# Seven block products in place of eight in two chunks of four input-projection units, with the sparse attention on two PSUM banks

## The chip, the cores and the metric

One core of a Trainium2 chip runs the whole program once. The time is the device time of that execution in microseconds (us). The engines named here are PE (TensorE, matrix products), DVE (VectorE), ACT (ScalarE), POOL (GpSimd) and SP (SyncE, which here only issues transfers).

## The reference

Two layers of a streaming encoder with 256 rows of width 2048, all in float32:

```python
for l in range(DEPTH):                       # DEPTH = 2, x is 256 x 2048
    h = rmsnorm(x, norm_mix[l])
    proj = h @ w_in[l]
    qa, ka, va, qi, ki, wi, qb, kb, vb = jnp.split(proj, offsets, axis=-1)
    o_a = dsa_branch(qa, ka, va, qi, ki, wi, bias_a)   # branch A: 8 heads x 128, top 64 keys chosen by an indexer
    o_b = swa_branch(qb, kb, vb, sinks[l], bias_b)     # branch B: 16 heads x 64, a window of 128 keys
    g_a, g_b = jnp.split(jax.nn.sigmoid(h @ w_gate[l]), 2, axis=-1)
    merged = g_a * (o_a @ w_branch_a[l]) + g_b * (o_b @ w_branch_b[l])
    x = x + merged @ w_out[l]
    h = rmsnorm(x, norm_mlp[l])
    x = x + jnp.square(jax.nn.relu(h @ w_up[l])) @ w_down[l]
return rmsnorm(x, final_norm)
```

The indexer scores each key as `sum over 16 heads of w * relu(q_idx . k_idx)`, and branch A attends to the 64 best of them.

## The kernel before

**Chunks and units.** Every weight matrix is cut into chunks of 256 rows (two blocks of 128) by 512 columns. Eight chunks make a unit: 512 output columns for all 256 rows of `x`, gathered in a pair of PSUM banks, `acc[s][0]` and `acc[s][1]`. A layer has 472 chunks: 8 narrow ones (`C_MISC`, index keys and the keys and values of branch B), 80 of the input projection (`C_WIN`, ten units), 48 + 48 of gates and branches, 32 of `w_out` and 256 of the MLP. I write "+n" for the chunk with number n counted from `C_WIN`; unit u of the input projection is +8u to +8u+7. Units 0 and 1 give the index queries, 2 and 3 the queries of branch A, 4 and 5 its keys, 6 and 7 its values, 8 and 9 the queries of branch B.

**A ring of four.** SP loads a chunk into `raw[c % 4]`, as soon as DVE has done chunk c-4. ACT rounds it to float32r (`w_hi`, `split`, L922) when PE has done chunk c-4; DVE subtracts for the rest (`w_lo`, L1350). PE multiplies: activations are kept as such a pair too, and each 128x128x512 product is three matmuls (hi x hi, hi x lo, lo x hi, L578 to L580), so a plain chunk is 12 matmuls of 512 columns. ACT and DVE thus run up to four chunks ahead of PE. All order is written out by hand; each engine runs its own list, and waits on counters.

**Seven products.** A "wide" chunk (`seven_products`, L546 to L548) treats the chunk as a 2x2 matrix of blocks times a 2x2 matrix of blocks and does seven products of 256 columns in place of eight, 21 matmuls in all. DVE first makes the sums of the weight blocks in `raw` (`weight_sums`, three instructions, L1359, L1363, L1365), placed one chunk ahead; then 1792 columns are rounded (`split_wide`, two on ACT, one on DVE, L1371). Sums of the activation blocks (`s_hh` and the like) have to be ready, and four of the seven products gather in two further banks; after the unit ACT copies a quarter (L1186 for the gates) and DVE makes five additions (`add_up_sides`, L1767 to L1775) that put the sides and `acc` together into `stage`. Before the change wide chunks are used in the gates of branch B and the MLP, 166 in all, and none in the input projection.

**Jobs.** Between chunks each engine does pieces of attention (`jobs_after`). A job that PE does after chunk c, ACT and DVE do after splitting chunk c+4 (`AHEAD`). Index scores come from `IDX_AT` on, the choice of keys (`choose`, DVE alone) from `TOPK_AT = C_WIN + 40`, the eight heads of branch A from `A_AT`, one each `A_STEP = 2` chunks: PE `a_logits` (L685), DVE `a_low`, ACT `a_exp` (L1020), DVE `a_probs` and `a_spread`, a transposition through HBM issued by POOL, ACT `a_take_probsT` (L1032), and three heads later PE `a_pv` (L698), ACT `a_o_hi` (L1038), DVE `a_o_lo` (L1571). `a_logits` uses banks `att[0]` and `att[1]` in turn, `a_pv` uses `att[2]`.

**Passing on.** Each of units 0 to 5 is scaled by ACT into `stage` (`take_win`, L1128, ahead of chunk 3 of the next unit), transposed in pieces of 32 by DVE (`spread_block`, L1428), stored to HBM by SP (L342), fetched back in four pieces (L348) and placed by ACT (`place`, L984, after chunk 6 of the next unit). Units 6 and 7 are scaled straight into `va`.

Of the kernel before, what the change touches and what calls it, by code (L numbers as in the profile page):

```python
# [11 lines left out]
P = 128  # L12
# [61 lines left out]
IDX_AT, IDX_STEP, IDX_ROUNDS = C_WIN + 24, 2, 6  # L74
TOPK_AT = C_WIN + 40
A_AT, A_STEP = C_WIN + 56, 2
# [14 lines left out]
GATES_WIDE = NBLK * len(WIDE_GATE)  # L91
G_SUMS = len(WIDE_GATE)
LAYER_WIDE = GATES_WIDE + (GROUPS - 1) * N_WIDE + len(WIDE_UP[2])
LAYER_SIDES = NBLK + 2 * (GROUPS - 1) + 1
U_SUMS = (GROUPS - 1) * NBLK
SHARED = ((0, 1, 2, 3, 4, 5, 8, 9), (-2, -1, 2, 3, 4, 5, 6, 7))
H_SUMS = 4
B11, B22, B21, T1, T3, T2, T4 = range(7)
# [15 lines left out]
def trunk_kernel(nc, x, w_misc, w_main, gains, sinks, rel_bias, onehot, final_gain, bias_rows, out):  # L114
    with ExitStack() as ctx:
# [11 lines left out]
        h_hl = sb("h_hl", [P, 2, KT, SEQ], F32R)  # L127
        o_hl = sb("o_hl", [P, 2, KT, SEQ], F32R)
# [73 lines left out]
        idx_banks = wide_acc  # L202
        first_turn = [acc[0][0], acc[0][1], acc[1][0], acc[1][1], turn, att[2], acc[0][0], acc[0][1]]
# [103 lines left out]
        def _(sp):  # L307
# [215 lines left out]
        def _(pe):  # L523
# [132 lines left out]

            def m_lhs(part, k, t):
                return o_lhs(part, k, t) if k < 8 else m_hl[:, part, k - 8, t * P:(t + 1) * P]


            def idx_scores(l, r):
                if r == 0:
                    pe.wait_ge(placed, l * E_M + (E_QK + 2))
                elif r >= 2:
                    pe.wait_ge(idx_relu, l * IDX_ROUNDS + (r - 1))
                t = 0 if r < 2 else 1
                keys = (t + 1) * P
                heads = NB // keys
                for i in range(heads):
                    for odd in range(2):  # L670
                        j = (r % 2 if t == 0 else r - 2) * heads + i
                        rows = slice(64 * odd, 64 * odd + 64)
                        last = nc.tensor.matmul(idx_banks[r % 2][odd][:, i * keys:(i + 1) * keys],
                                                qiT[rows, j, t * P:(t + 1) * P], kiT_kbT[rows, 0, 0:keys],
                                                start=(i == 0), stop=(i == heads - 1), skip_group_check=True)
                last.then_inc(idx_done, 1)

            def a_logits(l, h):
                if h == 0:
                    pe.wait_ge(placed, l * E_M + (E_QK + 6))  # L680
                    pe.wait_ge(idx_relu, (l + 1) * IDX_ROUNDS)
                if h >= 2:
                    pe.wait_ge(low_ready, l * JOBS + (h - 1))
                b = att[h % 2]
                nc.tensor.matmul(b[:, 0:P], qk[:, 0, h, 0:P], qk[:, 1, h, 0:P], start=True, stop=False, skip_group_check=True)  # L685
                nc.tensor.matmul(b[:, P:3 * P], qk[:, 0, h, P:SEQ], qk[:, 1, h, :], start=False, stop=True,
                                 skip_group_check=True).then_inc(logits_done, 1)

            def a_pv(l, h):
# [7 lines left out]
                b, pT = att[2], probsT[h % 2]  # L697
# [75 lines left out]
            for l in range(DEPTH):  # L773
# [19 lines left out]
                for u in range(N_WIN):  # L793
                    def win_between(c, u=u):
                        if l == 0 and u == 0 and c == 1:
                            spread_rows()
                        jobs_after(l, C_WIN + 8 * u + c)

                    def win_before(u=u):
                        if u >= 2:  # L800
                            pe.wait_ge(act_took, l * ACT_UNITS + (u - 1))
                    unit(l * CHUNKS + (C_WIN + 8 * u), 8, h_lhs, acc[u % 2], win_between, win_before)
# [75 lines left out]
                for g in range(GROUPS - 1):  # L878
                    up(g * 64 + (C_MLP + 16), 0, up_two_before(g), 2, [(1, h_sums_took, (G_SUMS + H_SUMS) * (l + 1))], WIDE_UP[2])
# [36 lines left out]
        def _(act):  # L916
# [119 lines left out]
            def a_o_hi(l, h):  # L1036
                act.wait_ge(pv_done, l * JOBS + (h + 1))
                nc.scalar.activation(o_hl[:, 0, h, :], att[2][:, 0:SEQ], ACT.Copy).then_inc(o_hi, 1)  # L1038
# [67 lines left out]
            for l in range(DEPTH):  # L1106
# [26 lines left out]

                def take_rows():
# [16 lines left out]
                for u in range(N_WIN):  # L1151
                    unit(l * CHUNKS + (C_WIN + 8 * u), 8,
                         take=(lambda u=u: take_win(u - 1)) if u else take_misc, taken=win_place(u),
                         jobs=win_jobs(u))
# [10 lines left out]
                def gate_sums_hi(n):  # L1165
                    act.wait_ge(h_summed, l * (G_SUMS + H_SUMS) + n + 1)
# [21 lines left out]
                def gate_tanh(n):  # L1188
                    act.wait_ge(up_summed, l * LAYER_SIDES + n + 1)
# [4 lines left out]
                def gate_steps(n):  # L1194
                    return lambda i: 3 * (l * LAYER_WIDE + n * len(WIDE_GATE) + i + 1)
# [11 lines left out]
                def h_sums(n):  # L1207
                    act.wait_ge(h_summed, l * (G_SUMS + H_SUMS) + G_SUMS + n + 1)
# [60 lines left out]
                def sides_count(g, i):  # L1269
                    return g * 2 + (l * LAYER_SIDES + NBLK + i + 1)  # L1270
# [72 lines left out]
        def _(dve):  # L1343
# [194 lines left out]
            def a_low(l, h):  # L1538
# [12 lines left out]
                low_of(att[h % 2], p, p[:, 0:P], 0, 0)  # L1551
                low_of(att[h % 2], p, p[:, P:3 * P], 1, 1).then_inc(low_ready, 1)
# [131 lines left out]
            for l in range(DEPTH):  # L1684
# [13 lines left out]

                for u in range(N_WIN):
                    take = take_keys if u == 0 else (lambda u=u: take_stage(u - 1)) if u <= 6 or u == 9 else None  # L1700
                    unit(l * CHUNKS + (C_WIN + 8 * u), 8, take=take, jobs=lambda c, u=u: jobs_after(l, C_WIN + 8 * u + c - AHEAD))
# [24 lines left out]
                def gate_sums(n):  # L1726

                    hi, lo = (h_hl[:, part, PIECES * n + 2:PIECES * n + 4, :].rearrange("p k s -> p (k s)").bitcast(F32)
                              for part in range(2))
                    both = stage2[:, 1, :]  # L1730
                    a11, a21, a12, a22 = (both[:, i * P:(i + 1) * P] for i in range(4))
                    s1, s2, s3, s4 = (sums_f[:, i * P:(i + 1) * P] for i in range(4))
                    chain.link(nc.vector.tensor_tensor(both, hi, lo, ALU.add))
                    nc.vector.tensor_tensor(s3, a21, a11, ALU.subtract)
                    chain.link(nc.vector.tensor_tensor(s1, a21, a22, ALU.add))
                    chain.link(nc.vector.tensor_tensor(s2, s1, a11, ALU.subtract))
                    nc.vector.tensor_tensor(s4, a12, s2, ALU.subtract).then_inc(h_summed, 1)

                def gate_sums_lo(n):
                    dve.wait_ge(h_sums_hi, l * (G_SUMS + H_SUMS) + n + 1)  # L1740
# [19 lines left out]
                def add_up_sides(g, n, i):  # L1760

                    z, w = wide_acc[n // 2]
                    at = g * 2 + (l * LAYER_SIDES + i)
                    steps = g * 6 + 3 * (l * LAYER_SIDES + i)
                    quarters = stage[:].rearrange("p t (h c) -> p (t h) c", h=2)
                    dve.wait_ge(sides_out, at + 1)
                    nc.vector.tensor_tensor(side_sum, z[:, 0:HALF], quarters[:, 1, :], ALU.add).then_inc(up_step, 1)  # L1767
                    dve.wait_ge(up_step, steps + 1)
                    nc.vector.tensor_tensor(quarters[:, 0::3, :], side_sum.unsqueeze(1).to_broadcast([P, 2, HALF]),
                                            w[:].rearrange("p (h c) -> p h c", h=2), ALU.subtract).then_inc(up_step, 1)  # L1770
                    dve.wait_ge(up_step, steps + 2)
# [56 lines left out]
                def h_sums(n):  # L1828
                    dve.wait_ge(h_sums_hi, l * (G_SUMS + H_SUMS) + G_SUMS + n + 1)
# [260 lines left out]
```

## Time and profile before

| | us |
|---|---|
| median of 3 runs (lowest to highest) | 2659.84 (2659.27 to 2660.45) |
| the profiled execution | 2658.03 |
| its span, first to last instruction | 2656.1 |
| PE busy in it | 2641.4 |
| DVE busy | 2078.8 |
| ACT busy | 1448.1 |
| granted TensorE clock | 0.999 |

The page shows one execution, with 1.9 us outside its span. A matmul's own duration (0.39 us for 512 columns) is longer than its distance from the next, because matmuls overlap in the array; what a chunk costs is read from start to start.

### The profile page before, as it was taken

To read this page: it belongs to the slowest core of one execution; us is meant where nothing else is said; L and a number is where in the kernel's file an instruction comes from. 1 tells how busy PE (TensorE), PEld (TensorE's weight loads), DVE (VectorE), ACT (ScalarE), POOL (GpSimd) and SP (SyncE) were. 2 spreads that over 40 slices of the span, in tenths; PEclk is the share of its full clock that TensorE was granted. 3 is DMA by queue.
4 is the path that set the end of the run, shared out by engine and by line. 5 is a ranking of instruction groups with operands and counts; after the bars stand their busy time and mean duration, and the time that the engine had idled before them with its cause. 6 is when DMAs were issued, how large, how long until landed. Compare 5 with 4: busy or idle time off the path is not lost.

```text
span 2656.1 us, 37301 instructions
## 1 busy us (share of the span) xinstructions
PE 2641.4 (99%) x13432; PEld 2217.1 (83%) x13432; DVE 2078.8 (78%) x3099; ACT 1448.1 (55%) x1863; POOL 215.8 (8%) x378
## 2 busy tenths in 40 slices
PE   9999999999999999999999999999999999999998
PEld 7788778888888888888888887788888888888887
DVE  5667678967898897987756766789678989989875
ACT  5445555545565655655455455555456556556554
POOL 0103110000100100100010021100000001000000
PEclk9999999999999999999999999999999999999999
DMA  7877676666775766767777666667677767667574
GB/s 260 239 236 224 222 226 195 229 231 231 244 228 191 246 216 206 240 205 232 235 237 225 224 225 221 218 202 233 227 256 231 221 208 242 209 217 234 189 248 151
DMA packets 187395, 594.52 MB, mean 224 GB/s; under 512 B 25576, under 2 KB 46612, under 8 KB 187088
## 3 DMA queue, kind: packets, MB, share of 16 engines
q1 hardware_dynamic: 166256, 536.94, 62.1%
q0 software_dynamic: 20432, 54.86, 7.5%
q8 instruction: 106, 1.74, 0.3%
q14 instruction: 73, 0.60, 0.1%
q10 hardware_dynamic: 528, 0.37, 0.1%
HBM read 544.58 MB, written 47.48 MB: 223 GB/s over the span
## 4 chain that ended last, share of the span: by engine, by line
PE 95%; DVE 3%; DMA 1%; issue 1%; ACT 0%; DVEq 0%; POOLq 0%; POOL 0%; SPq 0%; ACTq 0%
PE acc L578 24%; PE acc L579 24%; PE acc L580 24%; PE att L546 2%; PE att L548 2%; PE att L547 2%; PE acc L546 2%; PE acc L548 2%; PE acc L547 2%; PE acc L595 1%; PE acc L594 1%; PE acc L596 1%; DMA raw<-in_w_main 1%; DVE w_lo L1350 1%; DVE w_lo L1371 1%
## 5 line engine op out<-in xcount | busy, mean ns | idle before, releaser
L1350 DVE TENSOR_TENSOR w_lo<-raw,w_hi 128x1024 fp32r<-128x1024 f32 (+1 forms) x778 | 933.2, 1211 | 374.0 <-ACT w_hi L922 370.3
L922 ACT ACTIVATE w_hi<-raw 128x1024 fp32r<-128x1024 f32 (+1 forms) x778 | 813.1, 1051 | 633.5 <-PE acc L580 462.4
L578 PE MATMUL acc<-w_hi,h_hl 128*128 128x512 f32 x1848 | 735.2, 398 | 1.1 <-DVE w_lo L1350 1.1
L580 PE MATMUL acc<-w_hi,h_hl 128*128 128x512 f32 x1848 | 728.9, 394 | 0.0
L579 PE MATMUL acc<-w_lo,h_hl 128*128 128x512 f32 x1848 | 728.6, 394 | 0.0
L578 PEld LDWEIGHTS acc<-w_hi,h_hl 128*128 128x128 f32 x1848 | 347.9, 188 | 83.0 <-issue 4.9
L580 PEld LDWEIGHTS acc<-w_hi,h_hl 128*128 128x128 f32 x1848 | 347.9, 188 | 81.3
L579 PEld LDWEIGHTS acc<-w_lo,h_hl 128*128 128x128 f32 x1848 | 348.2, 188 | 76.3
L1371 DVE TENSOR_TENSOR w_lo<-raw,w_hi 128x1792 fp32r<-128x1792 f32 x166 | 335.5, 2021 | 33.5 <-ACT w_hi L931 32.4
L578 PE MATMUL acc<-w_hi,o_hl 128*128 128x512 f32 x912 | 360.4, 395 | 0.0
L579 PE MATMUL acc<-w_lo,o_hl 128*128 128x512 f32 x912 | 360.0, 395 | 0.0
L580 PE MATMUL acc<-w_hi,o_hl 128*128 128x512 f32 x912 | 359.6, 394 | 0.0
L929 ACT ACTIVATE w_hi<-raw 128x768 fp32r<-128x768 f32 x166 | 140.3, 845 | 195.0 <-PE acc L548 110.1
L931 ACT ACTIVATE w_hi<-raw 128x1024 fp32r<-128x1024 f32 x166 | 174.9, 1054 | 86.9 <-DVE raw L1365 86.7
L580 PEld LDWEIGHTS acc<-w_hi,o_hl 128*128 128x128 f32 x912 | 171.8, 188 | 40.2
L578 PEld LDWEIGHTS acc<-w_hi,o_hl 128*128 128x128 f32 x912 | 171.6, 188 | 37.7 <-issue 1.4
L579 PEld LDWEIGHTS acc<-w_lo,o_hl 128*128 128x128 f32 x912 | 171.7, 188 | 36.3
L1359 DVE TENSOR_TENSOR raw<-raw 128x512 f32<-128x512 f32 x166 | 113.3, 683 | 21.2 <-issue 11.3
L455 POOL DMA_DIRECT2D scratch<-spread x30 | 16.9, 563 | 973.2 <-DVE spread L1428 973.2
L1428 DVE STREAM_TRANSPOSE spread<-stage 128x512 f32<-128x512 f32 x112 | 73.0, 689 | 21.8 <-ACT stage L1128 17.5
L1020 ACT ACTIVATE probs<-probs,low 128x128 f32<-128x128 f32 x96 | 41.0, 428 | 85.0 <-DVE sink_d L1592 43.8
L1363 DVE TENSOR_TENSOR raw<-raw 128x256 f32<-128x256 f32 x166 | 70.6, 425 | 5.8
(298 smaller groups left out, 3614.9 us busy)
## 6 DMA issues: line engine op xcount, KB each, us to landing
raw<-in_w_main SPq DMA_DIRECT2D x928, 512.0 KB, 4.3
scratch<-spread SPq DMA_DIRECT2D x37, 512.0 KB, 2.8
moved<-scratch SPq DMA_DIRECT2D x148, 128.0 KB, 3.2
scratch<-spread POOLq DMA_DIRECT2D x30, 512.0 KB, 3.5
moved<-scratch POOLq DMA_DIRECT2D x120, 128.0 KB, 5.0
scratch_p<-spread POOLq DMA_DIRECT2D x16, 384.0 KB, 4.6
moved<-scratch_p POOLq DMA_DIRECT2D x64, 96.0 KB, 4.3
raw<-in_w_misc SPq DMA_DIRECT2D x16, 336.0 KB, 4.0
```

Of the source, the lines that this page charges most:

```text
L546: nc.tensor.matmul(o, a_hi, hi[:, w], start=start, stop=False, skip_group_check=True)
L547: nc.tensor.matmul(o, a_hi, lo[:, w], start=False, stop=False, skip_group_check=True)
L548: return nc.tensor.matmul(o, a_lo, hi[:, w], start=False, stop=stop, skip_group_check=True)
L578: nc.tensor.matmul(o, a_hi, hi[:, kk], start=(k == 0), stop=False)
L579: nc.tensor.matmul(o, a_hi, lo[:, kk], start=False, stop=False)
L580: last = nc.tensor.matmul(o, a_lo, hi[:, kk], start=False, stop=fin)
L922: nc.scalar.activation(w_hi[s][:, 0:2 * width], raw[r][:, 0:2 * width], ACT.Copy).then_inc(hi_ready, 1)
L929: nc.scalar.activation(w_hi[s][:, 0:3 * HALF], raw[s][:, HALF:CW], ACT.Copy)
L931: nc.scalar.activation(w_hi[s][:, 3 * HALF:7 * HALF], raw[s][:, CW:2 * CW], ACT.Copy).then_inc(hi_ready, 1)
L1350: nc.vector.tensor_tensor(w_lo[s][:, 0:2 * width], raw[r][:, 0:2 * width], w_hi[s][:, 0:2 * width].bitcast(F32), ALU.subtract).then_inc(lo ...
L1359: nc.vector.tensor_tensor(r[:, 4 * HALF:6 * HALF].rearrange("p (k n) -> p k n", k=2), r[:, HALF:3 * HALF].rearrange("p (k n) -> p k n", k= ...
L1371: nc.vector.tensor_tensor(w_lo[s][:, 0:7 * HALF], raw[s][:, HALF:8 * HALF], w_hi[s][:, 0:7 * HALF].bitcast(F32), ALU.subtract).then_inc(lo ...
```

## The change

Units 1, 2, 6 and 7 of the input projection (`WIN_UNITS`) do their chunks 1 and 5 (`WIN_CHUNKS`) as seven products: 8 chunks per layer, 16 in all. Their side products gather in `att[0]`, `att[1]` (units 1 and 6) and `att[2]`, `turn` (units 2 and 7). Since branch A would then meet unit 7's sides, its logits all use `att[0]` and its outputs `att[1]`; each `a_logits` so waits for the `low_ready` of the head before. The index scores begin four chunks later, the heads of branch A two chunks later. Unit 0 gets the sums of the activations (`gate_sums`, moved ahead in the file, and `win_sums_lo`). The results of units 1 and 2 are spread after chunk 5 of the next unit in place of ahead of chunk 3, and passed on and placed in the unit after it. The index keys, `best8`, the activation sums and a side sum lie in the half of `o_hl` that is not yet used, since `raw1` now needs its full width.

```diff
-IDX_AT, IDX_STEP, IDX_ROUNDS = C_WIN + 24, 2, 6
+IDX_AT, IDX_STEP, IDX_ROUNDS = C_WIN + 28, 2, 6
-A_AT, A_STEP = C_WIN + 56, 2
+A_AT, A_STEP = C_WIN + 58, 2
+WIN_UNITS = (1, 2, 6, 7)
+WIN_CHUNKS = (1, 5)
...
+        s_win = o_hl[:, :, 10:14, :].rearrange("p a k s -> p a (k s)").rearrange("p a (b c) -> p a b c", b=W_SUMS)
...
+        win_sides = dict(zip(WIN_UNITS, (wide_acc[0], wide_acc[1], wide_acc[0], wide_acc[1])))
...
# SP, for each unit u
+                    if u - 2 in WIN_UNITS[0:2]:
+                        store, fetch = pass_on(l, E_QK + u - 2)
+                        then = {1: [store], 2: [fetch]}
+                    load_unit(l, C_WIN + 8 * u, 8, None if u - 1 in WIN_UNITS[0:2] else passing, then=then)
...
# PE
+                    pe.wait_ge(up_summed, l * LAYER_SIDES + 2)          # idx_scores, first round
...
-                if h >= 2:
-                    pe.wait_ge(low_ready, l * JOBS + (h - 1))
-                b = att[h % 2]
+                    pe.wait_ge(up_summed, l * LAYER_SIDES + 3)          # a_logits, h == 0
+                else:
+                    pe.wait_ge(low_ready, l * JOBS + h)
+                b = att[0]
...
-                b, pT = att[2], probsT[h % 2]
+                b, pT = att[1], probsT[h % 2]
...
+                    hold = {1: [(1, misc_took, l + 1), (1, h_sums_took, l * LAYER_SUMS + 1), (5, h_sums_took, l * LAYER_SUMS + 2)],
+                            2: [(1, rows_out, 1)], 6: [(1, idx_relu, (l + 1) * IDX_ROUNDS)]}
...
# ACT
+                def win_side(u):
+                    unit_done(l * CHUNKS + (C_WIN + 8 * (u + 1)))
+                    act.wait_ge(spread_ready, l * MOVES + (E_QK + min(u, 6)))
+                    nc.scalar.activation(stage[:, 0, HALF:NB], win_sides[u][0][:, HALF:NB], ACT.Copy).then_inc(sides_out, 1)
+
+                def win_scale(u):
+                    act.wait_ge(up_summed, l * LAYER_SIDES + WIN_UNITS.index(u) + 1)
+                    for t in range(TT):
+                        dst = stage[:, t, :] if u < 6 else va[:, t, (u - 6) * NB:(u - 5) * NB]
+                        last = nc.scalar.activation(dst, stage[:, t, :], ACT.Copy, scale=rms[:, 2 if u == 2 else 0, t:t + 1])
+                    last.then_inc(act_took, 1)
...
+                    if u == 0:
+                        then = {5: lambda: win_sums_hi(0), 7: lambda: win_sums_hi(1)}
+                    if was_wide:
+                        then[4] = lambda u=u: win_scale(u - 1)
+                    if u - 2 in WIN_UNITS[0:2]:
+                        then[0] = win_place(u - 1)
...
# DVE
+                    if u == 0:
+                        then = {4: lambda: gate_sums(0), 6: first_lo_second_sums}
+                    if u == 1:
+                        then = {0: lambda: win_sums_lo(1)}
+                    if u - 1 in WIN_UNITS:
+                        then[3] = lambda u=u: add_win_sides(u - 1)
+                        if u <= 6:
+                            then[5] = take
+                        take = None
```

`then[k]` is done after the split of chunk k of the unit.

**What moves on ACT around unit 7 and the heads of branch A.** Names: `w_hi` is a split, `probs` a head's exponentials (two rows a head), `probsT` the transposed probabilities of an earlier head, `o_hl<-att` an output of `a_pv`, `qiv` the values. Before, from the last rows of one head to the next:

```order
L1020 ACTIVATE probs,den<-probs,low 128x256
L1032 ACTIVATE probsT<-moved_a 128x384
L922 ACTIVATE w_hi<-raw 128x1024 x2
L1038 ACTIVATE o_hl<-att 128x256
L1020 ACTIVATE probs,den<-probs,low 128x128
L1020 ACTIVATE probs,den<-probs,low 128x256
L1032 ACTIVATE probsT<-moved_a 128x384
L1128 ACTIVATE qiv<-acc,rms 128x512 x2
```

and of the changed kernel, the same heads:

```order
L1055 ACTIVATE probsT<-moved_a 128x384
L1160 ACTIVATE stage<-att 128x256
L945 ACTIVATE w_hi<-raw 128x1024 x2
L1166 ACTIVATE qiv<-stage,rms 128x512 x2
L1061 ACTIVATE o_hl<-att 128x256
L1043 ACTIVATE probs,den<-probs,low 128x128
L1043 ACTIVATE probs,den<-probs,low 128x256
L1055 ACTIVATE probsT<-moved_a 128x384
```

The copy of the side (L1160) and the scaling of unit 7's values (L1166) now stand inside the chain of head 3: ahead of its output copy, its exponentials and head 1's `probsT`.

**What moves on DVE at the same place.** Names: `w_lo` a split, `win_side_sum` and `stage` the five additions of a side, `o_hl<-att` an output of branch A. Before, ahead of head 3:

```order
L1566 STREAM_TRANSPOSE stage<-probs 128x3x4x32
L1350 TENSOR_TENSOR w_lo<-raw,w_hi 128x1024 x2
L1571 TENSOR_TENSOR o_hl<-att,o_hl 128x256
L1545 TENSOR_TENSOR probs<-bias_a,score 128x128
L1546 TENSOR_TENSOR probs<-bias_a,score 128x256
```

and changed, up to the head's output and first row (head 3 goes on behind it as before):

```order
L1617 STREAM_TRANSPOSE stage<-probs 128x3x4x32
L1401 TENSOR_TENSOR w_lo<-raw,w_hi 128x1024
L1782 TENSOR_TENSOR win_side_sum<-att,stage 128x256
L1784 TENSOR_TENSOR stage<-win_side_sum,turn 128x2x256
L1787 TENSOR_TENSOR stage<-stage,turn 128x256
L1788 TENSOR_TENSOR stage<-acc,stage 128x512
L1790 TENSOR_TENSOR stage<-acc,stage 128x512
```

The five additions stand between the two splits that lead to head 3.

**What moves on ACT in units 2 and 3.** `qiv<-moved` is the placing of index queries. Before, it stands after seven splits of the unit that follows, here with the taking of the unit ahead of it:

```order
L1128 ACTIVATE stage<-acc,rms 128x512 x2
L922 ACTIVATE w_hi<-raw 128x1024 x4
L984 ACTIVATE qiv<-moved 128x1024
L922 ACTIVATE w_hi<-raw 128x1024 x4
```

and of the changed kernel, for the second of the two:

```order
L1160 ACTIVATE stage<-att 128x256
L945 ACTIVATE w_hi<-raw 128x1024 x2
L1166 ACTIVATE stage<-stage,rms 128x512 x2
L952 ACTIVATE w_hi<-raw 128x768
L954 ACTIVATE w_hi<-raw 128x1024
L945 ACTIVATE w_hi<-raw 128x1024 x3
L1007 ACTIVATE qiv<-moved 128x1024
```

Six chunks are now split between the unit's end and the placing, two more than the four before.

## Rows read from the trace of the kernel before

**Rows 1.** The page: the span, the engines' busy time.
```profile
span 2656.1 us, 37301 instructions
PE 2641.4 (99%) x13432; PEld 2217.1 (83%) x13432; DVE 2078.8 (78%) x3099; ACT 1448.1 (55%) x1863; POOL 215.8 (8%) x378
```
**Rows 2.** Waits of PE: us in total, times, longest.
```profile
PE acc L578 <- DVE w_lo L1350: 1.1, 1, 1.1
```
**Rows 3.** PE in order of time (start, duration): a wide chunk, then a plain one.
```profile
725.87 0.28 PE L546 MATMUL att<-w_hi,s_hh 128*128 128x256 f32 x1
...
728.35 0.39 PE L578 MATMUL acc<-w_hi,h_hl 128*128 128x512 f32 x1
...
731.13 0.28 PE L546 MATMUL att<-w_hi,s_hh 128*128 128x256 f32 x1
```
**Rows 4.** One form of weight load on PE: ns min/median/max, first and last start.
```profile
L546 PEld LDWEIGHTS att<-w_hi,s_hh x182: 186/188/192, 419.2 to 2533.1; 128*128 128x128 f32 x182
```
**Rows 5.** Split of one plain chunk (+4 of layer 0): ACT, DVE, PE.
```profile
53.60 1.06 ACT L922 ACTIVATE w_hi<-raw 128x1024 fp32r<-128x1024 f32 x1 [0.65 <-PE acc L580]
54.70 1.22 DVE L1350 TENSOR_TENSOR w_lo<-raw,w_hi 128x1024 fp32r<-128x1024 f32 x1 [0.24 <-ACT w_hi L922]
61.74 0.40 PE L578 MATMUL acc<-w_hi,h_hl 128*128 128x512 f32 x1
```
**Rows 6.** DVE in a gate unit: additions of the sides, weight sums, split, wide split.
```profile
440.40 0.42 DVE L1767 TENSOR_TENSOR stage<-att,stage 128x256 f32<-128x256 f32 x1
...
443.11 0.68 DVE L1359 TENSOR_TENSOR raw<-raw 128x512 f32<-128x512 f32 x1
...
444.63 1.22 DVE L1350 TENSOR_TENSOR w_lo<-raw,w_hi 128x1024 fp32r<-128x1024 f32 x1
446.28 2.02 DVE L1371 TENSOR_TENSOR w_lo<-raw,w_hi 128x1792 fp32r<-128x1792 f32 x1 [0.44 <-ACT w_hi L931]
```
**Rows 7.** ACT there: copy of the side, scaling of the unit.
```profile
437.90 0.39 ACT L1186 ACTIVATE stage<-att 128x256 f32<-128x256 f32 x1 [1.36 <-PE acc L548]
...
443.23 1.34 ACT L1191 ACTIVATE stage<-stage,rms 128x512 f32<-128x512 f32 x2 [1.43 <-DVE stage L1775]
```
**Rows 8.** DVE, ACT and PE in branch A, layer 0, by time.
```profile
209.72 0.39 PE L578 MATMUL acc<-w_hi,h_hl 128*128 128x512 f32 x1
210.00 0.08 DVE L1535 DVE_READ_ACCUMULATOR2_ANT low<- 128x1 f32 x1
212.50 2.58 DVE L1350 TENSOR_TENSOR w_lo<-raw,w_hi 128x1024 fp32r<-128x1024 f32 x2
215.00 0.42 DVE L1571 TENSOR_TENSOR o_hl<-att,o_hl 128x256 fp32r<-128x256 f32 x1
217.56 0.51 ACT L1032 ACTIVATE probsT<-moved_a 128x384 f32<-128x384 f32 x1
219.39 0.59 PE L698 MATMUL att<-probsT,qiv 128*128 128x256 f32 x2
```
**Rows 9.** Passing on: transposition on DVE (page); slowest and fastest of twelve passes.
```profile
L1428 DVE STREAM_TRANSPOSE spread<-stage 128x512 f32<-128x512 f32 x112 | 73.0, 689 | 21.8 <-ACT stage L1128 17.5
...
1392.57 0.33 SPq L342 DMA_DIRECT2D scratch<-spread  x1
1403.41 1.06 ACT L984 ACTIVATE qiv<-moved 128x1024 f32<-128x1024 f32 x1 [3.99 <-DMA moved<-scratch]
1465.91 0.33 SPq L342 DMA_DIRECT2D scratch<-spread  x1
1473.81 1.06 ACT L984 ACTIVATE qk<-moved 128x1024 f32<-128x1024 f32 x1 [1.05 <-DMA moved<-scratch]
```
**Rows 10.** DVE and PE at the choice of keys, unit 6.
```profile
176.09 1.23 DVE L1350 TENSOR_TENSOR w_lo<-raw,w_hi 128x1024 fp32r<-128x1024 f32 x1
182.66 0.39 PE L578 MATMUL acc<-w_hi,h_hl 128*128 128x512 f32 x1
```
**Rows 11.** Busy time by stretch (us, then PE, PEld, DVE, ACT, POOL).
```profile
416.00:560.00 144.00, 144.00 (x785) 124.38 (x784) 126.94 (x144) 77.04 (x84) 3.53 (x1) 1.00 0.68 223
```

More of the change, by code:

```diff
@@ L1037, in a_o_hi @@
                 act.wait_ge(pv_done, l * JOBS + (h + 1))
-                nc.scalar.activation(o_hl[:, 0, h, :], att[2][:, 0:SEQ], ACT.Copy).then_inc(o_hi, 1)
+                nc.scalar.activation(o_hl[:, 0, h, :], att[1][:, 0:SEQ], ACT.Copy).then_inc(o_hi, 1)
             def b_exp(l, j):
@@ L1151, in _ @@
                 for u in range(N_WIN):
+                    was_wide, then = u - 1 in WIN_UNITS, {}
+                    if u == 0:
[4 more added lines that the diff above has]
+                        then[0] = win_place(u - 1)
                     unit(l * CHUNKS + (C_WIN + 8 * u), 8,
-                         take=(lambda u=u: take_win(u - 1)) if u else take_misc, taken=win_place(u),
-                         jobs=win_jobs(u))
+                         take=(lambda u=u: win_side(u - 1)) if was_wide else (lambda u=u: take_win(u - 1)) if u else take_misc,
+                         taken=None if u - 1 in WIN_UNITS[0:2] else win_place(u), jobs=win_jobs(u), then=then,
+                         wide=WIN_CHUNKS if u in WIN_UNITS else (),
+                         steps=early_steps(WIN_UNITS.index(u)) if u in WIN_UNITS else None)
                 def take_gate(cl_end, branches):
@@ L1697, in take_stage, with gate_sums @@
                     spread_block(l, E_QK + u if u < 6 else E_QB + u - 8, stage)
+                def gate_sums(n):
+                    hi, lo = (h_hl[:, part, PIECES * n + 2:PIECES * n + 4, :].rearrange("p k s -> p (k s)").bitcast(F32)
+                              for part in range(2))
+                    both = stage2[:, 1, :]
+                    a11, a21, a12, a22 = (both[:, i * P:(i + 1) * P] for i in range(4))
+                    s1, s2, s3, s4 = (sums_f[:, i * P:(i + 1) * P] for i in range(4))
+                    chain.link(nc.vector.tensor_tensor(both, hi, lo, ALU.add))
+                    nc.vector.tensor_tensor(s3, a21, a11, ALU.subtract)
+                    chain.link(nc.vector.tensor_tensor(s1, a21, a22, ALU.add))
+                    chain.link(nc.vector.tensor_tensor(s2, s1, a11, ALU.subtract))
+                    nc.vector.tensor_tensor(s4, a12, s2, ALU.subtract).then_inc(h_summed, 1)
@@ L1724, in take_branch_b @@
                     spread_block(l, E_M + n, stage2)
[L1726 to L1737, printed above, removed]
                 def gate_sums_lo(n):
-                    dve.wait_ge(h_sums_hi, l * (G_SUMS + H_SUMS) + n + 1)
+                    dve.wait_ge(h_sums_hi, l * LAYER_SUMS + W_SUMS + n + 1)
                     nc.vector.tensor_tensor(s_hh[:, 1, n, :], sums_f, s_hh[:, 0, n, :].bitcast(F32), ALU.subtract)\
```

103 lines of the change are left out of this document (67 added, 36 removed).

## Prediction

> **What bounds the kernel now.** I first read the page's busy times [rows 1]: the reader is to see that PE is busy for 2641.4 us of a span of 2656.1, and DVE for 2078.8. PE sets the time, and DVE is the engine nearest behind it. Then PE's waits [rows 2]: in the whole span it once waited for a split, for 1.1 us. So work taken from PE is a gain at once, and work given to DVE or ACT costs nothing until PE meets something that isn't ready. The rest of the reading was to find where that happens: what a chunk costs PE [rows 3], how far ahead its split is ready [rows 5], and what stands in series in the places where the order moves [rows 6 to 10].
>
> **What PE saves.** A wide chunk lasts from 725.87 to 728.35, 2.48 us, the plain one behind it from 728.35 to 731.13, 2.78 to 2.79 [rows 3]. I use 2.79, so 0.31 is saved. Four units with two such chunks in two layers are 16 chunks: 16 x 0.31 = 4.96 us. That is 0.19% of the time, and this measurement can tell about 0.2% (5.3 us) from no change. So even with the whole gain the kernel would hardly be told to be faster.
>
> A wide chunk has 21 matmuls in place of 12, so nine more weight loads. Such a load lasts 0.188 us [rows 4], and 21 of them would be 3.95 us in a row, more than the 2.48 us that the whole chunk lasts [rows 3]: they lie beside the matmuls. The Trainium skill ("TensorE: Matmul & The Clock Gate", section "Measured speedup vs the span model") says that a weight load overlaps matmuls in flight only when its row group differs; all of these loads use all 128 rows. By that rule the nine loads would stand in series, 16 x 9 x 0.188 = 27 us more, and the change would lose some 22 us. The trace disagrees, by the two durations above.
>
> **What is added beside PE.** On DVE: the sums of the weight blocks 1.52 us per wide chunk (443.11 to 444.63), the wide split 2.02 in place of 1.22, so 0.80, and the additions of the sides 2.71 per unit (440.40 to 443.11) [rows 6]. On ACT: a copy of 0.39 per unit; the scaling, 1.34, was there before, and moves from the unit's end to behind the additions [rows 7]. The activation sums of unit 0 are new work for DVE and ACT, about 2.7 us twice and 0.4 us twice by rows of such sizes (two or three operations like those of rows 6, one like that of rows 7).
>
> A normal split is ready long before its use: that of chunk +4 ends at 55.92, and PE starts the chunk at 61.74, 5.8 us later [rows 5]. It can hardly be earlier, since a slot comes free only when PE is done with it. So at each place there is a cover of up to 5.8 us, and an addition below it is free. For unit 0 and for the first wide chunks that holds with 2 to 3 us left, and I cost them at nothing. In the stretch of gate units that are built in this way, DVE is busy for 126.94 of 144.00 us and PE for all 144.00 [rows 11]: such a load alone doesn't stall PE. What can is a place where several things stand in series. I find three.
>
> **Place A: head 3 and unit 7's sides.** Zero is PE's start of the chunk after which it does the first output of branch A: 209.72 before [rows 8]. Before, by those rows: DVE starts the two splits at +2.78 (212.50), head 0's output is at +5.28 (215.00), and the `probsT` of head 1 is ready at +8.35 (217.56 + 0.51). PE comes for it at +9.67 (219.39). The margin is 1.32 us. In the changed order unit 7's sides, scaling and all, stand ahead of that `probsT`:
> - DVE comes 0.7 late from the wide chunk and the sides ahead of it. That is a choice: 1.52 + 0.80 + 0.31 = 2.63 are added there, and there are idle stretches that take up most of it; between 0 and 1.5.
> - ACT's copy of the side, 0.39, ahead of the split: it starts at 2.78 + 0.7 + 0.39 = 3.87, and ends 1.2 later at 5.07.
> - Five additions, 2.71: 7.78. ACT's scaling waits for them, 1.34: 9.1. Behind it on ACT stands the output copy of head 0, which DVE waits for, 0.39 by the copy of the same size: 9.5.
> - From that output on the order is as before, 8.35 - 5.28 = 3.07: `probsT` is ready at 12.6.
>
> PE comes at 9.67 (the three chunks up to there are plain in both), so it waits 2.9 us, in each of two layers: +5.8. The bounds are those of the lateness: with 0 it is 2.2, with 1.5 it is 3.7 per layer. Behind ACT's late instructions the splits of the next chunks queue as well, but their cover is larger, and PE itself is held. Head 4's logits stand on PE behind this wait, so their new wait for head 3's `low` (on DVE about 1.3 us behind the output, 10.9) costs nothing further.
>
> **Place B: index queries placed late.** Zero is PE's start of +16, the first chunk of unit 2. DVE does the additions of unit 1 up to about 5.5 (ACT copies the side and rounds +19, DVE splits it until 2.8, then 2.71), weight sums to 7.0, the split of +20 to 8.2, the wide split of +21 to 10.65, and the two transpositions (2 x 0.689 [rows 9]) to 12.0. Then the pass through HBM: from SP's store to ACT's placing it took 7.9 us in the fastest (1465.91 to 1473.81) and 10.84 in the slowest (1392.57 to 1403.41) [rows 9]. I take 9.5, near the middle: 21.5. The placing is 1.06, and behind it on ACT stands the rounding of +25, 1.06, then DVE's split, 1.22 [rows 5]: 24.8. PE wants +25 at 6 x 2.79 + 2 x 2.48 + 2.79 = 24.49. So about 0.4 us per layer, with bounds of 0 (a pass of 7.9) and 1.7 (one of 10.84): +0.8. Unit 2's own placing is one unit later, where no wide chunk hastens PE; its cover is larger, and I cost it at nothing.
>
> This pass is a store and a fetch. The Trainium skill ("DMA: Bandwidth & Descriptors", section "Anatomy of one DMA — SWDGE (gpsimd) path") gives about 2 us of fixed cost for a transfer, two of them 4 us; by an estimate from that, place B would have no wait at all and the sum would be 0.8 lower. The fastest pass of this trace, 7.9 us, disagrees, so I go by the rows.
>
> **Place C: the choice of keys.** Here DVE has no gap. Its split ends at 177.32 and PE starts the chunk at 182.66: 5.34 left [rows 10]. Unit 6 adds 2 x (1.52 + 0.80) = 4.64 ahead of it, PE comes 0.31 earlier, and the scores are some 0.1 later: 0.3 is left. I take 0.1 per layer, +0.2, with bounds of 0 and, if DVE comes 1 us late from the unit before, 0.7.
>
> **The sum.** -4.96 + 5.8 + 0.8 + 0.2 = +1.84. The profiled execution lasted 2658.03, of which 1.9 lie outside the span, and would become 2659.9. The median is 1.8 above that execution, 2659.84, and becomes 2661.7. With places A to C at their lower bounds the sum is -4.96 + 4.4 = -0.6 (2659.3), at their upper -4.96 + 7.4 + 3.4 + 1.4 = +7.2 (2667.1).
>
> **The rivals.**
> - The whole gain: no wait surfaces, 2659.84 - 4.96 = 2654.9. For it speaks that in the gate units DVE carries the same load with no stall of PE [rows 11]; against it that head 3's chain has but 1.32 us of margin [rows 8], and 4.5 us are put into it. It would need DVE and ACT to have idle time in this chain that I haven't seen.
> - The slower side: DVE comes to unit 6 and unit 8 about 1.5 us later than I take it, because between +48 and +66 it gets 2 x 2.71 + 4 x 2.32 = 14.7 us more work beside the choice of keys, which has no gaps. Then A costs 3.7 and C 0.7 or more per layer, and with B at the upper half (1.0) the sum is -4.96 + 7.4 + 1.4 + 2.0 = +5.8, with a split or two more that come late about +7: 2667. It decides from about 1 us of lateness at +53.
> - One bank for the logits: each head's logits wait for the `low` of the head before. Before, head 2's was read at 210.08, and the next logits could come at the earliest after the chunk, at 209.72 + 2.79 = 212.51 [rows 8], so 2.43 us of margin. If DVE were later than that at every head, by 0.5 us say, the 14 such waits would cost 7 us: 2668.7. Against it: the lateness of 0.7 doesn't use the margin up.
> - Weight loads in series, as above, some 2682: the rows speak against it.
>
> **How the numbers follow.** The forecast, waits at A of about 2.9 and small ones at B and C, has 0.56, with its own range of 2659.3 to 2664.5. The whole gain, or most of it, has 0.14; DVE behind by more 0.21; the logits' wait 0.06; loads or anything unlike these 0.03. Faster by over 0.2% is below 2654.5: even the whole gain ends just above it, so 0.06, from the first rival. Slower by over 0.2% is above 2665.2: most of the second and third, and the edge of the forecast, 0.26. Within it 0.68. The range is 2655.2 to 2668: it leaves out a little of each side.
>
> **What would show it.** In the profile after, a wide chunk of the input projection should last 2.48 us. PE should wait at `a_pv` of head 1 for ACT's `probsT`, twice, 2.9 us each; a wait of under 1 us there makes place A wrong, and with it the forecast. At +25 it should wait for `w_lo` by 0 to 1.7, at +53 by 0 to 0.7. DVE's busy time should grow by 16 x 2.32 + 8 x 2.71 + 4 x 2.7 = 70 us, to some 2149. PE waits at other splits of units 6 to 8 would speak for the second rival, and waits of the logits for `low` for the third.

## The result, and the profile after

| | before | changed |
|---|---|---|
| median (lowest to highest), us | 2659.56 (2656.28 to 2661.04), 6 runs | 2678.11 (2675.30 to 2681.02), 6 runs |
| profiled execution's span | 2656.1 | 2678.5 |
| PE busy | 2641.4 | 2648.8 |
| DVE busy | 2078.8 | 2141.5 |
| granted TensorE clock | 0.999 | 0.997 |

The ratio is 1.0071, 95% interval 1.0059 to 1.0082: slower, by 18.6 us. Forecast were 2661.7 and a range up to 2668.0.

The page of the changed kernel, against [rows 1]:

```profile
span 2678.5 us, 37743 instructions
PE 2648.8 (99%) x13576; PEld 2226.0 (83%) x13576; DVE 2141.5 (80%) x3211; ACT 1461.4 (55%) x1891; POOL 215.7 (8%) x378
```

The span grew by 22.4 us. PE's idle time in it grew from 14.7 (2656.1 - 2641.4) to 29.7, so by 15.0, and its busy time by 7.4, though 4.96 us of work were to go. So PE also ran slower somewhere. PE's waits, in us, times, longest (answers to [rows 2]):

```profile
PE acc L593 <- DVE w_lo L1401: 6.0, 6, 3.0
PE att L718 <- ACT probsT L1055: 5.4, 2, 2.7
PE att L692 <- ACT stage L1037: 4.4, 3, 1.8
...
PE att L561 <- DVE w_lo L1422: 1.2, 2, 0.9
```

The second row is place A of the prediction. The first is mostly place B: 4.7 of its 6.0 us are two waits, at +25 of each layer; of the other four the longest is 0.5. The third is in no step of it: L692 are the index scores, waiting for ACT to take the round before out of the banks. Here are PE's rows at the five waits of units 3 and 4 (chunks +25, +32, +36 of layer 0, +25 and +36 of layer 1), the bracket telling the idle time and its releaser:

```profile
100.86 0.51 PE L593 MATMUL acc<-w_hi,h_hl 128*128 128x512 f32 x1 [1.65 <-DVE w_lo L1401]
...
128.48 0.48 PE L692 MATMUL att<-kiT_kbT,qiv 64*128 64x256 f32 x1 [1.80 <-ACT stage L1037]
...
145.27 0.48 PE L692 MATMUL att<-kiT_kbT,qiv 64*128 64x256 f32 x1 [1.70 <-ACT stage L1037]
...
1430.25 0.79 PE L593 MATMUL acc<-w_hi,h_hl 128*128 128x512 f32 x1 [3.05 <-DVE w_lo L1401]
...
1471.76 0.48 PE L692 MATMUL att<-kiT_kbT,qiv 64*128 64x256 f32 x1 [0.92 <-ACT stage L1037]
```

Together 9.1 us. Why, ACT's rows of the same stretch say (start, duration, bracket as above):

```profile
97.54 1.06 ACT L1007 ACTIVATE qiv<-moved 128x1024 f32<-128x1024 f32 x1 [8.03 <-DMA moved<-scratch]
98.51 1.99 ACT L945 ACTIVATE w_hi<-raw 128x1024 fp32r<-128x1024 f32 x2
...
122.18 1.06 ACT L1007 ACTIVATE qk<-moved 128x1024 f32<-128x1024 f32 x1 [8.74 <-DMA moved<-scratch]
123.15 1.07 ACT L1037 ACTIVATE stage<-att 128x512 f32<-128x512 f32 x2
...
143.19 1.06 ACT L1007 ACTIVATE qk<-moved 128x1024 f32<-128x1024 f32 x1 [5.09 <-DMA moved<-scratch]
144.15 0.58 ACT L1037 ACTIVATE stage<-att 128x512 f32<-128x512 f32 x1
```

L1007 is the placing, of units 1, 2 and 3. ACT stands at it for 8.03, 8.74 and 5.09 us, and what is queued behind it is what PE wants: first the split of +25, then twice the take of index scores (L1037). In the kernel before the first take was done at 99.45, nine us ahead of unit 2's placing:

```profile
99.45 1.09 ACT L1014 ACTIVATE stage<-att 128x512 f32<-128x512 f32 x2
...
108.93 1.06 ACT L984 ACTIVATE qk<-moved 128x1024 f32<-128x1024 f32 x1 [1.71 <-DMA moved<-scratch]
```

For units 1 and 2 SP's rows show the store and, behind a chunk's load, the fetch (4 pieces), in layer 0:

```profile
86.36 0.33 SPq L353 DMA_DIRECT2D scratch<-spread  x1
...
90.73 1.75 SPq L359 DMA_DIRECT2D moved<-scratch  x4
...
110.61 0.33 SPq L353 DMA_DIRECT2D scratch<-spread  x1
...
116.19 1.75 SPq L359 DMA_DIRECT2D moved<-scratch  x4
```

From store to placing that is 11.18 and 11.57 us.

And PE ran slower behind some of these waits. The stretches behind those of 128.48 and 145.27, and one between them (PE busy and count, PEld, DVE, ACT, POOL, then the granted clock, DMA share, GB/s):

```profile
130.00:134.00 4.00, 4.00 (x13) 3.08 (x12) 3.75 (x10) 2.56 (x4) 0.60 (x1) 0.62 0.93 278
134.00:138.00 4.00, 4.00 (x19) 3.25 (x18) 3.89 (x6) 2.02 (x2) 0.60 (x1) 1.00 0.78 271
147.00:150.00 3.00, 3.00 (x8) 2.30 (x7) 2.96 (x4) 1.20 (x3) 0.26 (x1) 0.50 0.21 50
```

A clock of 0.50 is TensorE at its lower level, 1.2 GHz. From start to start, chunk +33 then took 4.45 us, +37 4.44, and +25 of layer 1 4.39, where 2.89 is normal behind such jobs: 4.6 us for three chunks. Behind the wait of 1.65 at +25 of layer 0 the chunk took its normal 2.89.

Place A, with PE, ACT and DVE by time (answers to [rows 8]; PE's start of +64 is at 224.25):

```profile
229.56 0.41 DVE L1782 TENSOR_TENSOR win_side_sum<-att,stage 128x256 f32<-128x256 f32 x1
231.67 0.68 DVE L1790 TENSOR_TENSOR stage<-acc,stage 128x512 f32<-128x512 f32 x1
232.39 1.34 ACT L1166 ACTIVATE qiv<-stage,rms 128x512 f32<-128x512 f32 x2 [3.05 <-DVE stage L1790]
234.03 0.42 DVE L1622 TENSOR_TENSOR o_hl<-att,o_hl 128x256 fp32r<-128x256 f32 x1 [0.55 <-ACT o_hl L1061]
236.59 0.51 ACT L1055 ACTIVATE probsT<-moved_a 128x384 f32<-128x384 f32 x1
237.15 0.70 PE L718 MATMUL att<-probsT,qiv 128*128 128x256 f32 x2 [2.71 <-ACT probsT L1055]
```

The output of head 0 is at +9.78 (forecast 9.5), `probsT` at +12.85 (12.6), and PE waits 2.71 in layer 0 and 2.64 in layer 1 (2.9). PE itself came later too, at +10.2 (9.67), so two small misses cancel in part.

### The profile page after: what moved, and what is told of

It is laid out like the page before. It is cut to its first block, busy times and chain, and to the rows that moved or that the text cites. A ratio compares the mean times of both kernels' runs of the same rounds, so it can differ in the third digit from the quotient of the medians.

```text
span 2678.5 us, 37743 instructions
## 1 busy us (share of the span) xinstructions
PE 2648.8 (99%) x13576; PEld 2226.0 (83%) x13576; DVE 2141.5 (80%) x3211; ACT 1461.4 (55%) x1891; POOL 215.7 (8%) x378
## 4 chain that ended last, share of the span: by engine, by line
PE 75%; DVE 12%; DMA 6%; issue 4%; ACT 2%; SPq 1%; POOL 0%; DVEq 0%; POOLq 0%; ACTq 0%
PE acc L593 18%; PE acc L595 18%; PE acc L594 18%; DVE w_lo L1401 4%; DMA raw<-in_w_main 2%; PE att L561 2%; PE att L563 2%; PE att L562 2%; DMA moved<-scratch 2%; PE acc L561 2%; PE acc L563 2%; PE acc L562 2%; DMA scratch<-spread 2%; DVE w_lo L1422 1%; PE acc L611 1%
## 5 line engine op out<-in xcount | busy, mean ns | idle before, releaser
L1401 DVE TENSOR_TENSOR w_lo<-raw,w_hi 128x1024 fp32r<-128x1024 f32 (+1 forms) x762 | 912.4, 1210 | 312.7 <-ACT w_hi L945 310.9
L945 ACT ACTIVATE w_hi<-raw 128x1024 fp32r<-128x1024 f32 (+1 forms) x762 | 793.0, 1050 | 539.8 <-PE acc L595 348.6
L593 PE MATMUL acc<-w_hi,h_hl 128*128 128x512 f32 x1784 | 712.5, 399 | 6.3 <-DVE w_lo L1401 6.0
L595 PE MATMUL acc<-w_hi,h_hl 128*128 128x512 f32 x1784 | 705.4, 395 | 0.0
L594 PE MATMUL acc<-w_lo,h_hl 128*128 128x512 f32 x1784 | 705.3, 395 | 0.0
L593 PEld LDWEIGHTS acc<-w_hi,h_hl 128*128 128x128 f32 x1784 | 336.9, 189 | 87.9 <-DVE w_lo L1401 9.0
L595 PEld LDWEIGHTS acc<-w_hi,h_hl 128*128 128x128 f32 x1784 | 336.9, 189 | 79.0
L1422 DVE TENSOR_TENSOR w_lo<-raw,w_hi 128x1792 fp32r<-128x1792 f32 x182 | 367.9, 2021 | 30.8 <-ACT w_hi L954 30.0
L952 ACT ACTIVATE w_hi<-raw 128x768 fp32r<-128x768 f32 x182 | 153.7, 845 | 201.5 <-PE acc L563 102.2
L954 ACT ACTIVATE w_hi<-raw 128x1024 fp32r<-128x1024 f32 x182 | 191.9, 1055 | 108.7 <-DVE raw L1416 108.5
L1410 DVE TENSOR_TENSOR raw<-raw 128x512 f32<-128x512 f32 x182 | 124.3, 683 | 33.9 <-DMA raw<-in_w_main 22.2
L1414 DVE TENSOR_TENSOR raw<-raw 128x256 f32<-128x256 f32 x182 | 77.4, 425 | 6.3
L1416 DVE TENSOR_TENSOR raw<-raw 128x256 f32<-128x256 f32 x182 | 77.4, 425 | 6.3
```

The costliest lines, as they stand in the source:

```text
L593: nc.tensor.matmul(o, a_hi, hi[:, kk], start=(k == 0), stop=False)
L594: nc.tensor.matmul(o, a_hi, lo[:, kk], start=False, stop=False)
L595: last = nc.tensor.matmul(o, a_lo, hi[:, kk], start=False, stop=fin)
L945: nc.scalar.activation(w_hi[s][:, 0:2 * width], raw[r][:, 0:2 * width], ACT.Copy).then_inc(hi_ready, 1)
L952: nc.scalar.activation(w_hi[s][:, 0:3 * HALF], raw[s][:, HALF:CW], ACT.Copy)
L954: nc.scalar.activation(w_hi[s][:, 3 * HALF:7 * HALF], raw[s][:, CW:2 * CW], ACT.Copy).then_inc(hi_ready, 1)
```

## The experiments

My theory (theory 1): most of the loss comes from the placings on ACT, which stand ahead of splits and index takes while the transfer isn't there, and from the clock that falls behind the waits. The rival (theory 2): it comes from the index rounds being four chunks later, or from DVE being behind with its new work. The kernel before ran beside each; its medians were 2658.69 in the first four, 2659.67 in the others.

**e1, placings later on ACT.**

```diff
-                        then[0] = win_place(u - 1)
+                        then[2 if u == 3 else 3] = win_place(u - 1)
```

> The changed kernel with one edit: ACT places the output of unit 1 after split +26 in place of +24, and that of unit 2 after split +35 in place of +32. Theory 1 (ACT stands at the placing, waiting for a transfer, and the splits and index takes queued behind it come late; TensorE's clock falls behind the pauses): the waits near +25, +32 and +36 and the low clock behind them go, 14.6 us in both layers of the trace after, so about 2663.5 us. Theory 2 (the index rounds themselves, four chunks later, meet unit 3's transfer and the scores on DVE): only the waits at +25 go, about 6 us, so 2672 us, and waits for the index takes stay.

Measured: 2666.9 us (2661.15 to 2672.83), ratio 1.0035 (1.0024 to 1.0046), so 11.2 us less than the changed kernel, or 10.3 if each is compared with the kernel before that ran beside it. The execution with the profile was the fastest of the seven; what the slower ones waited for isn't shown. Its waits:

```profile
PE att L718 <- ACT probsT L1055: 5.8, 3, 2.7
...
PE acc L593 <- DVE w_lo L1401: 1.1, 2, 0.8
PE att L692 <- ACT stage L1037: 1.0, 1, 1.0
```

Waits for splits fell from 6.0 to 1.1 us (both that are left stand behind the input projection), those for the takes from 4.4 to 1.0, at +36, behind unit 3's placing, which this edit leaves where it was. No chunk of units 3 and 4 ran at the lower clock. The first take now stands ahead of unit 2's placing, and the transfer has come when ACT gets there (no bracket on L1007):

```profile
109.29 1.09 ACT L1037 ACTIVATE stage<-att 128x512 f32<-128x512 f32 x2
...
120.84 1.06 ACT L1007 ACTIVATE qk<-moved 128x1024 f32<-128x1024 f32 x1
```

The gain alone doesn't decide: 10 to 11 us lie between the 14.6 of theory 1 and the 6 of theory 2. The waits do, in this trace: theory 2 wanted those for the takes to stay, and they went but for one.

**e2, the index rounds alone, four chunks later, in the kernel before.**

```diff
-IDX_AT, IDX_STEP, IDX_ROUNDS = C_WIN + 24, 2, 6
+IDX_AT, IDX_STEP, IDX_ROUNDS = C_WIN + 28, 2, 6
```

> The kernel before with one edit: the index rounds begin at +28 in place of +24. Theory 1: no wait of PE for the takes, 2659 to 2661 us. Theory 2: PE waits for them at +32 or +36 in each layer, and the clock falls behind it, 4 to 8 us slower than before.

Measured: 2659.51, ratio 1.0001 (0.9993 to 1.001), and no wait of PE for the takes in its trace. The shift alone costs nothing; theory 2 in its first form falls.

**e3, unit 7's additions out of head 3's chain.**

```diff
 # DVE, unit 8
-                        then[3] = lambda u=u: add_win_sides(u - 1)
+                            gaps = {5: lambda: add_win_sides(7, (0,)), 7: lambda: add_win_sides(7, (1,))}
 # ACT
-                        then[4] = lambda u=u: win_scale(u - 1)
+                        then[7 if u == 8 else 4] = lambda u=u: win_scale(u - 1)
```

`gaps` is done ahead of the split of that chunk; part 0 is the first three additions, part 1 the last two.

> The changed kernel with unit 7's five additions out of head 3's chain: three on DVE ahead of split +69, two ahead of +71, the scaling on ACT after split +71. If place A is what the prediction says, PE's wait for probsT (2 x 2.7 us) goes, and 2673 us are left. Rival: DVE and ACT are behind in general there, and the wait moves to another head; no gain.

Measured: 2676.68 (2672.77 to 2682.52), ratio 1.006 (1.0047 to 1.0073): 1.4 us less than the changed kernel, within the spread of both. In the trace:

```profile
PE acc L593 <- DVE w_lo L1401: 7.6, 5, 2.7
PE att L692 <- ACT stage L1037: 5.5, 3, 3.9
PE att L718 <- ACT probsT L1055: 3.6, 4, 1.6
```

The wait behind +66 is gone, but two others stand in its place in each layer, 0.2 behind +68 and 1.6 behind +70. I had moved the scaling ahead of the split of +72, and so into another head's chain. The two upper rows, mostly of units 3 and 4, were longer in this execution, the slowest of the five, than in that of the changed kernel and hide what was won.

**e4, both edits.**

> Both edits together. Theory 1: 14.6 + 5.4 us less than the changed kernel, 2658 us, within 0.2% of the kernel before, on the faster side of it if nothing new waits. Theory 2: some 2666 us.

Measured: 2662.43, ratio 1.0014 (1.0006 to 1.0023), 4.5 us less than e1. What is left in its trace is PE's wait for `probsT` at `a_pv` (3.7 us in five) and, in layer 1, a placing that I hadn't touched, unit 0's. ACT stood at it for 7.25 us, and PE waited 1.78 and 1.68 us for the splits behind it, +15 and +16.

**e5, e4 with ACT's order mended further.** The scaling of unit 7 goes ahead of split +73, and the placings of units 0 and 3 go one split back, behind the index takes:

```diff
+                    if u in (1, 4):
+                        then[7] = win_place(u)
...
+                         at={1: lambda: win_scale(7)} if u == 9 else (),
```

> The kernel with both edits (placings later, unit 7's additions in the gaps), and two more: the scaling of unit 7 on ACT ahead of split +73 in place of after +71, and the placings of units 0 and 3 one split later, behind the index takes. If ACT's order in these places is all that is left, the waits at pv after +70 (1.8 us in each layer), at +36 (1.0 to 1.3) and at +15 go, some 6 us less than 2662.4: 2656 to 2657, ratio 0.999. If DVE is what is late in branch A, the wait at pv stays and the time with it, 2660 or more.

Measured: 2662.57, ratio 1.001 (1.0001 to 1.0019). That missed: I expected 2656 to 2657, and what came is the outcome that I had given for DVE being late in branch A. The waits at the takes and the 1.6 behind +70 are gone, but the heads now wait a little each:

```profile
PE att L718 <- ACT probsT L1057: 2.9, 8, 0.7
```

The one chain that I measured in branch A has 1.32 us to spare [rows 8]. That unit 7's 2.71 + 1.34 us fit into none of them, cut up or not, is how I read it, after two other orders of that work (that of e3 and e4, and that of e5). Which engine is late first isn't shown, since e3 moves work on ACT and on DVE at once.

**e6, seven products in units 1 and 2 alone; e7, in units 6 and 7 alone.**

```diff
-WIN_UNITS = (1, 2, 6, 7)
+WIN_UNITS = (1, 2)       # e6, with A_AT = C_WIN + 56
+WIN_UNITS = (6, 7)       # e7, with IDX_AT = C_WIN + 24 and units 1, 2 passed on as before
```

> The changed kernel with seven products in units 1 and 2 alone (units 6 and 7 plain, branch A's heads back at +56, one bank for the logits as in the changed kernel). Theory 1 (the late placings carry the loss): -2.5 us of PE and the whole of the waits and the slow clock at +25 to +37, 14.6 us: about 2671 us. Rival (DVE behind in units 6 to 8 carries it): no more than 2662 us. If one bank for the logits costs something, waits of the logits for DVE's low show.

Measured: 2671.37 (2666.23 to 2673.48), ratio 1.0043 (1.0029 to 1.0057), as theory 1 has it. Its waits are those of units 3 and 4 alone; the logits, which use one bank here too, wait nowhere:

```profile
PE att L692 <- ACT stage L1036: 8.0, 3, 3.4
PE acc L593 <- DVE w_lo L1400: 4.4, 2, 2.2
```

> The changed kernel with seven products in units 6 and 7 alone, units 1 and 2 plain and passed on and placed as before the change, index rounds from +24. Theory 1: -2.5 us, and +5.8 of the wait at place A and nothing else: about 2662 us, ratio 1.0012. Rival: waits at the splits of unit 6 and more, 2668 us.

Measured: 2667.42, ratio 1.0035 (1.0021 to 1.0048). No wait but the forecast one was to come, and in the input projection only one other did, 0.35 us at the first `a_pv`, yet the time is 5 us above what I expected. PE's row behind the wait and the stretch around it:

```profile
227.36 1.22 PE L717 MATMUL att<-probsT,qiv 128*128 128x256 f32 x2 [2.72 <-ACT probsT L1054]
```

```profile
226.00:230.00 4.00, 2.64 (x9) 2.37 (x9) 3.00 (x6) 3.47 (x8) 0.58 (x1) 0.61 0.07 30
```

The same wait as in the changed kernel (2.72 against 2.71), the same matmuls: 1.22 us here, 0.70 there. The clock fell, and chunk +66 with its jobs took 4.1 us more than before in place of 3.0, in both layers. Twice 4.1, less 2.5 for eight wide chunks, makes 5.7 of the 7.8 between the medians. PE's two waits for splits of over 0.5 us, 1.7 together, stand in the MLP of layer 1, which this edit doesn't touch and where the kernel before has one of 1.09, so they say nothing of units 6 and 7:

```profile
1823.10 0.51 PE L593 MATMUL acc<-w_hi,h_hl 128*128 128x512 f32 x1 [0.76 <-DVE w_lo L1400]
...
2080.32 0.39 PE L561 MATMUL att<-w_hi,m_hl 128*128 128x256 f32 x1 [0.89 <-DVE w_lo L1421]
```

**e8, e6 with the placings later.**

> Units 1 and 2 alone, with ACT's placings after split +26 and +35. Theory 1: the waits at +25, +32 go, 2656 to 2659 us, as the kernel before or 2 us faster. Rival (the transfers themselves are late and keep PE waiting wherever they are placed): 2665 us or more.

Measured: 2659.0, ratio 1.0 (0.9991 to 1.0009), 12.4 us less than e6. PE's waits for takes and splits are down to 0.6 and 0.6 us. The 0.6 for a take stands at +36, behind the placing of unit 3, and the 0.6 for a split in the MLP. The one edit of e1, in a kernel with no other trouble, takes away the loss of units 1 and 2. Of the 2.5 us that eight wide chunks save 0.7 show in the medians, with an interval of 2.4 to either side. The rival (transfers that are late wherever they are placed) falls.

**e9, units 1, 2 and 6, with all four placings later; e10, the same with the heads from +56.**

```diff
-WIN_UNITS = (1, 2, 6, 7)
+WIN_UNITS = (1, 2, 6)
-A_AT, A_STEP = C_WIN + 58, 2        # e10 only
+A_AT, A_STEP = C_WIN + 56, 2
```

> Seven products in units 1, 2 and 6 (unit 7 plain, so no additions stand in a head's chain), ACT's placings later as in e1, those of units 0 and 3 one split later too, heads from +58. By what the runs so far showed no wait of PE over 1 us should be left in units 2 to 8, and 12 wide chunks save 3.7 us: 2655 to 2656 us, ratio 0.9986. If what is left over in units 6 to 8 comes from DVE's load and not from unit 7's sides, waits at pv stay and the time is 2659 or more.

Measured: 2656.52 (2652.65 to 2657.43), ratio 0.9989 (0.9980 to 0.9998): faster than both kernels, by 0.1% against the kernel before, with an interval that ends just short of no change. In units 1 to 9 PE waits for nothing. Its page:

```profile
span 2650.7 us, 37641 instructions
PE 2637.4 (99%) x13540; PEld 2219.6 (84%) x13540; DVE 2129.2 (80%) x3189; ACT 1460.6 (55%) x1885; POOL 215.8 (8%) x378
```

The whole list of its waits:

```profile
PE att L593 <- DVE h_hl L1464: 1.9, 1, 1.9
PE acc L544 <- DMA xs<-in_x: 1.5, 1, 1.5
PE att L785 <- DVE moved L1705: 1.3, 1, 1.3
PE att L593 <- DVE w_lo L1403: 0.3, 1, 0.3
```

PE's busy time is 4.0 below before [rows 1], where 12 chunks by 0.31 make 3.7. So the wide chunks save what was worked out, once nothing waits; the medians differ by 3.2.

> The same with branch A's heads from +56 as before the change. If the first head has to wait for unit 6's additions, it costs 0.5 to 2 us per layer against e9 (2656 to 2660); if not, the same as e9.

Measured: 2664.01, ratio 1.0018 (1.0008 to 1.0027), 7.5 us above e9; I had given 0.5 to 2 per layer. The first head's logits wait for unit 6's additions, 2.7 in each layer, and the clock falls behind that too:

```profile
195.26 0.46 PE L705 MATMUL att<-qk 128*128 128x128 f32 x2 [2.69 <-DVE stage L1792]
```

```profile
194.00:198.00 4.00, 2.74 (x8) 2.28 (x9) 3.42 (x10) 1.84 (x5) 0.00 (x0) 0.70 0.57 168
```

Chunk +57 then took 4.36 us in layer 0 and 4.52 in layer 1, where 2.98 is normal with its jobs. Waiting makes 5.4 us and the clock some 2.9; the sum, 8.3, is near the 7.5 between the medians.

## Why the prediction was wrong, step by step

- **What PE saves, 4.96 us: right.** The wide chunks of the input projection last 2.48 to 2.53 us in the trace after where no head's job stands before them, and in e9 PE's busy time fell by the whole saving. That weight loads lie beside matmuls holds too. (The rule of the Trainium skill that the prediction sets against it stands in "TensorE: Matmul & The Clock Gate", section "The mechanism", and not in the section that the prediction names.) DVE's busy time grew by 62.7 us, where 70 were forecast.
- **Place A, 2.9 us of waiting per layer: right** in the chain (12.85 for 12.6) and the wait (2.71 and 2.64), with PE 0.5 us later than I had it. Its price can be higher than the wait: in e7 it was 4.1 per layer, by the clock.
- **Place C, the choice of keys: right.** The split of +53 was ready 0.50 us ahead of PE in layer 0 (forecast 0.3), and PE didn't wait for it. In e5 and e10 it waited there once, 0.4 and 0.2 us, within the bounds.
- **Place B, 0.4 us per layer: the mechanism was right and the size off.** It was 1.65 and 3.05. The passes took 11.18 (store at 86.36, placing at 97.54) and 11.31 us, outside of the 7.9 to 10.84 of [rows 9], where I had taken 9.5. In layer 1 the store also came later, 13.1 us after PE's start of +16 in place of 12.0; ACT had stood for 6.42 us at the placing of unit 0 before, and that this is the reason isn't shown. The estimate beside it, 4 us for a store and a fetch, takes a figure that the Trainium skill ("DMA: Bandwidth & Descriptors", section "Anatomy of one DMA — SWDGE (gpsimd) path") gives for transfers issued by GpSimd. Here SP issues them, and the six passes of units 1 to 3 took 8.4 to 11.6 us.
- **"Unit 2's own placing is one unit later ...; its cover is larger, and I cost it at nothing": this step failed.** Of what is queued behind the waiting placing I had looked at the splits alone. But ACT's take of the index scores stands there too, ahead of the split, and PE's next round waits for it; before, the take came first. With a pass of 11.57 us in layer 0 unit 2's placing became late, and PE waited 1.80 us for a take. The takes, begun four chunks later, then met unit 3's placing as well, which is in no step at all: 1.70 and 0.92 us. The later start alone costs nothing (e2), and in layer 1 unit 2's pass took 9.44 us and made no wait. e1 and e8 took nearly all of these waits away by placing units 1 and 2 later (1.05 and 0.61 are left, at +36 of layer 0), and e9, which also places unit 3 behind the takes, has none.
- **The clock was in no term of the sum.** Three chunks behind waits cost 4.6 us more. With the two failures above: 4.4 (takes) + 3.9 (place B, 4.7 less 0.8) + 4.6 = 12.9 us. By the starts of PE's chunks the input projection of the two layers took 17.0 us more in the profiled execution (10.1 and 6.9), 15.1 more than the sum's +1.84. The 12.9 are most of that; a chunk also grew by 0.1 to 0.3 us more than the wait in it (+36 of layer 0 by 1.95 for 1.70).
- **What stands outside.** The same execution took 1.9 us more in the very first chunk, and 0.5 and 2.7 behind the two projections, in chunks that the change doesn't touch; in the last of these stretches PE waited 2.1 us for splits, where it was 1.1 before. In the first chunk the matmuls began 0.28 us apart in place of 0.15, with a granted clock shown as 1.00. It was so in e2, e3, e5 and e8 too (+1.8 to +2.3), and not in the other traces, the kernel before among them. So two single executions can differ by 2 us with no cause in the change; what decides between the two starts stays open.
- **The rivals.** "DVE behind by more" didn't show: in units 5 to 9 PE waited for no split, neither in the changed kernel nor with units 6 and 7 alone (e7). The most that showed of it is place C in e5 and e10, 0.4 and 0.2 us. The wait of the logits for one bank never showed (e6, e8).

## What to carry to other kernels

When a step that waits for a transfer is moved on an in-order engine, list everything behind it until its data has come, and for each the engine that waits: the small copy out of PSUM behind it can matter more than the big split. Move such a step behind them where its result isn't needed yet; here that cost nothing (e8, e9). And price a wait of the matrix engine by the chunk behind it too, not by the wait alone.

## What the runs showed of the hardware

A wait of PE can cost more than its length, since the granted clock falls to its lower level for about one chunk behind it: +1.4 to +1.6 us (e10, and +33 and +37 of the changed kernel, behind waits of 1.7 to 3.05). It doesn't follow from the wait's length: behind the 2.71 us at place A of the changed kernel the next chunk took 2.97, as before, behind the 2.72 of e7 the clock was at 0.61; behind 1.65 at +25 nothing fell, behind 1.70 and 1.80 in the index rounds it did. In e6 the clock was at 0.58 in the 4 us behind a wait of 2.33 (layer 0, +32), and at 1.00 behind another of 2.33 (layer 1, +36). What decides it stays open.
